# Prompt attention of a hybrid decoder step: a looped pass per KV head becomes one unrolled run of sixteen query tiles, and the softmax factors move from the transposes to the closed sums

## The reference, cut to what matters

```python
o_c, p_grp = compressed_attention(q, kc, vc, pos)     # 63 summary blocks, those that end before the token
o_s = selected_prompt(q, kv_s, idx, pos)              # 16 selected blocks of 64: with 1024 tokens, all of them
o_w = window_prompt(q, kv_w)                          # the last 512 tokens, a band
o = gates[..., 0:1] * o_c + gates[..., 1:2] * o_s + gates[..., 2:3] * o_w
```

## Time and profile before

| what | value |
|---|---|
| median of 3 runs | 3282.19 us (3277.84 to 3283.11) |
| the profiled execution, its own time | 3281.28 us |
| its span in the profile | 3279.6 us |
| TensorE busy in the span | 2924.5 us, 89% |
| VectorE, ScalarE, GpSimd busy | 44%, 28%, 9% |
| the stage that changes, first turn to last addition | 474.8 us, from 1623.5 to 2098.3 |
| its granted TensorE clock, mean | 0.86 |

### The profile page before, as it was taken

The page is one execution under the profiler, slowest core; times in us unless marked ns, Lnnn a source line. Parts: engine busy times, 40 slices in busy tenths (PEclk is TensorE's granted clock), DMA queues, the critical chain, the costliest instruction groups (busy, mean ns, idle before and its releaser), DMA issues. The chain is left out here.

```text
span 3279.6 us, 48743 instructions
## 1 busy us (share of the span) xinstructions
PE 2924.5 (89%) x18374; PEld 2688.3 (82%) x18374; DVE 1448.3 (44%) x2808; ACT 905.5 (28%) x1537; POOL 311.1 (9%) x294
## 2 busy tenths in 40 slices
PE   4999989999999997885789789687799999999997
PEld 4889879999999996884667667433589999999996
DVE  4444455544444445013255456312326454444445
ACT  4665651111111102111245345233222111111112
POOL 3444410000000001000011011211000000000000
PEclk9999999999999998997579879888899999999999
DMA  4212133211111102102100000365322111111101
GB/s 158 110 56 110 62 105 105 64 38 38 40 50 42 47 0 87 33 26 77 35 1 1 2 1 1 125 183 158 112 58 62 42 53 49 38 38 51 38 13 53
DMA packets 168574, 193.84 MB, mean 59 GB/s; under 512 B 11431, under 2 KB 154536, under 8 KB 165679
## 3 DMA queue, kind: packets, MB, share of 16 engines
q1 hardware_dynamic: 161623, 141.58, 14.2%
q0 software_dynamic: 6816, 50.49, 4.2%
HBM read 178.30 MB, written 17.91 MB: 60 GB/s over the span
## 5 line engine op out<-in xcount | busy, mean ns | idle before, releaser
L407 ACT ACTIVATE f_act_gate<-f_act_gate 128x352 f32<-128x352 f32 x132 | 65.8, 498 | 1186.2 <-DVE f_act_gate L464 1186.1
L501 DVE SCALAR_TENSOR_TENSOR trunk<-f_down,trunk 128x352 f32<-128x352 f32 x528 | 275.8, 524 | 207.8 <-PE f_down L104 207.8
L102 PE MATMUL f_up<-f_h_hi,f_gu_hi 128*128 128x352 f32 x1056 | 344.6, 326 | 0.0
L102 PE MATMUL f_gate<-f_h_hi,f_gu_hi 128*128 128x352 f32 x1056 | 344.3, 326 | 0.0
L104 PE MATMUL f_up<-f_h_hi,f_gu_lo 128*128 128x352 f32 x1056 | 342.8, 325 | 0.0
L104 PE MATMUL f_gate<-f_h_hi,f_gu_lo 128*128 128x352 f32 x1056 | 342.5, 324 | 0.0
L102 PE MATMUL f_down<-f_a_hi,f_wd_hi 128*128 128x352 f32 x1056 | 340.6, 323 | 0.0
L103 PE MATMUL f_gate<-f_h_lo,f_gu_hi 128*128 128x352 f32 x1056 | 340.5, 322 | 0.0
L103 PE MATMUL f_up<-f_h_lo,f_gu_hi 128*128 128x352 f32 x1056 | 340.1, 322 | 0.0
L103 PE MATMUL f_down<-f_a_lo,f_wd_hi 128*128 128x352 f32 x1056 | 338.5, 321 | 0.0
L104 PE MATMUL f_down<-f_a_hi,f_wd_lo 128*128 128x352 f32 x1056 | 338.1, 320 | 0.0
(11 more groups left out here) (333 smaller groups left out, 5812.3 us busy)
## 6 DMA issues: line engine op xcount, KB each, us to landing
as_pages<-in_cache_kv_slc_dram SPq DMA_DIRECT2D x192, 128.0 KB, 2.3
f_gu_raw<-in_w_ffn_gate_dram SPq DMA_DIRECT2D x44, 512.0 KB, 4.5
f_gu_raw<-in_w_ffn_up_dram SPq DMA_DIRECT2D x44, 512.0 KB, 5.7
f_wd_raw<-in_w_ffn_down_dram SPq DMA_DIRECT2D x22, 1024.0 KB, 5.0
as_pages<-in_cache_kv_slc_dram POOLq DMA_DIRECT2D x64, 128.0 KB, 3.2
in_w_raw<-in_w_in_dram SPq DMA_DIRECT2D x4, 1304.0 KB, 5.9
x_saved<-trunk SPq DMA_DIRECT2D x1, 4224.0 KB, 16.2
trunk<-x_saved SPq DMA_DIRECT2D x1, 4224.0 KB
```

What stands on the lines that cost most here:

```text
L102: pe.matmul(out, w_hi, x_hi, start=first, stop=False)
L407: act.activation(act_gate[:, b, :], act_gate[:, b, :], ACT.Silu).then_inc(silu_done, 1)
L501: dve.scalar_tensor_tensor(xT[:, m, chunk(c)], down_bank[n % 4][:, 0:CH], 0.5, xT[:, m, chunk(c)], ALU.mult, ALU.add).then_inc(down_free, 1)
```

## The change

The stage is written out for all sixteen tiles `n = 8 g + qt` (`TILES`) without a loop; waits have constant values and the `nop`s are gone. Beyond that:

- **Turns without factors.** A value turn is a transpose of `probs` with the identity. `diag` and GpSimd's `diagonals` are gone, and so is the wait for them.
- **Branches summed apart.** The products of the selected, window and compressed units of a tile go to `out_bank[(3 n + b) % 2]`, each closed on its own. Each closed sum is multiplied by its factors with VectorE (`scale`, one 128x512 product for each branch) into `scaled`, and GpSimd adds the three and the two halves into `mixT` (`gather`). `take_upper` and `take` are gone.
- **Factor rows.** The factors are per query, but in the closed sums queries lie along the free axis. `factors` is done once for a tile in the first head step of the next one; the 12 factors are split high and low (`factor_split`), transposed to 24 rows (turn `("f", n, None)`), and for each branch `b` four matmuls with `pick` (built once by GpSimd) spread the right rows over all partitions (turn `("f", n, b)`), which ScalarE copies to `spread`. These four turns a tile go through the same two turn banks. They stand in the first head step of the next tile (at its end) and at the head of its steps 1, 2 and 3.
- **Order.** A head's selected scores are issued at the end of the head step before, then comes the first turn of the step with the product still pending, then the window scores, then the other turns. ScalarE does the window exponentials after all the turns of the step. VectorE does the first `low` between the two maxima.
- **The seam.** The key and query turns of the second KV head alternate with the first units of tile 7 (`lead`), and the rest of tile 7's units lie in the head steps of tile 8.

```diff
-                with pe.Fori(0, N_KV) as g:
+    def lead(n):
+        own = [("k", n, b, half) for b in range(2) for half in range(2)] + [("q", n)]
+        values = quarter(n - 1, 0) if n else []
+        mixed = [x for pair in zip(own, values) for x in pair]
+        return mixed + own[len(values):]
+
+    def turns(n, r):
+        own = [("q", n + 1)] if r == 2 and n + 1 < TILES and not leads(n + 1) else []
+        if n == 0:
+            return own
+        values = [] if r == 0 and leads(n) else quarter(n - 1, r)
+        if r == 0:
+            return values + [("f", n - 1, None)]
+        return [("f", n - 1, r - 1)] + own + values
+
+    def head(xs):
+        return xs[:1] if xs and xs[0][-1] is not None else []
...
+                def gather(n):
+                    g, qt = divmod(n, QT)
+                    pool.wait_ge(scaled_done, 3 * n + 2)
+                    pool.tensor_tensor(scaled[:, 0], scaled[:, 0], scaled[:, 1], ALU.add).then_inc(added, 1)
+                    pool.wait_ge(scaled_done, 3 * n + 3)
+                    pool.wait_ge(added, 4 * n + 1)
+                    pool.tensor_tensor(scaled[:, 0], scaled[:, 0], scaled[:, 2], ALU.add).then_inc(added, 1)
+                    pool.wait_ge(added, 4 * n + 2)
+                    pool.tensor_copy(upper[:], scaled[HD:2 * HD, 0]).then_inc(added, 1)
+                    pool.wait_ge(added, 4 * n + 3)
+                    for half, sem in enumerate((added, out_taken)):
+                        pool.tensor_tensor(mixT[half * HD:(half + 1) * HD, 2 * g:2 * g + 2, qt * P:(qt + 1) * P],
+                                           scaled[0:HD, 0, half::2, :], upper[:, half::2, :], ALU.add).then_inc(sem, 1)
...
+                        for x in first:
+                            high(x)
+                        if n < TILES:
+                            exp_selected(n, r)
+                        for x in rest:
+                            high(x)
+                        if n < TILES:
+                            exp_window(n, r)
...
+                def scale(n, b):
+                    dve.wait_ge(pv_done, products[("v", n, ends[n][b])] + 1)
+                    dve.wait_ge(hi_done, at[("f", n, b)] + 1)
+                    if n:
+                        dve.wait_ge(out_taken, n)
+                    dve.tensor_tensor(scaled[:, b], out_bank[(3 * n + b) % 2][:].rearrange("p (r n) -> p r n", r=GROUP),
+                                      spread[:, b], ALU.mult).then_inc(scaled_done, 1)
...
                         for h in range(GROUP):
-                            tr = pe.matmul(bank[0:rows, h * P:(h + 1) * P], probs[qt % 2][:, h, lo:lo + rows],
-                                           diag[:, qt % 2, h, branch, :], start=True, stop=True)
+                            tr = pe.transpose(bank[0:rows, h * P:(h + 1) * P], probs[n % 2][:, h, lo:lo + rows],
+                                              K["ident"][:])
...
+                        _, n, b = x
+                        pe.wait_ge(hi_done, at[("f", n, None)] + 1)
+                        if n == 0 and b == 0:
+                            pe.wait_ge(pick_ready, 1)
+                        for h in range(GROUP):
+                            tr = pe.matmul(bank[:, h * P:(h + 1) * P], pick[:, 3 * h + BRANCHES[b], :], factor_rows[:],
+                                           start=True, stop=True)
...
+                def through(x):
+                    turn(x)
+                    value_product()
+                    if x[0] == "v":
+                        pending.append(x)
+
+                for n in range(TILES + 1):
+                    for r in range(GROUP):
+                        xs = turns(n, r)
+                        first = lead(n) if r == 0 and leads(n) else head(xs)
+                        rest = xs if r == 0 and leads(n) else xs[len(first):]
+                        for x in first:
+                            through(x)
+                        if r == 0 and leads(n):
+                            selected_scores(n, r)
+                        if n < TILES:
+                            window_scores(n, r)
+                        for x in rest:
+                            through(x)
+                        following = (n, r + 1) if r + 1 < GROUP else (n + 1, 0)
+                        if following[0] < TILES and not (following[1] == 0 and leads(following[0])):
+                            selected_scores(*following)
+                value_product()
```

More of the change, by code:

```diff
@@ L1608, in value_units @@
                 + [(CMP, CMP0, NB, None)])
[L1610 to L1637, removed]
+    def quarter(n, r):
+        count = len(value_units(n))
+        return [("v", n, u) for u in range(count * r // GROUP, count * (r + 1) // GROUP)]
@@ new lines, in head @@
+    def head(xs):
+        return xs[:1] if xs and xs[0][-1] is not None else []
+    order = [x for n in range(TILES + 1) for r in range(GROUP)
+             for x in (lead(n) if r == 0 and leads(n) else []) + turns(n, r)]
+    at = {x: i for i, x in enumerate(order)}
+    dups = {x: i for i, x in enumerate([x for x in order if x[0] in "kq"])}
+    dup_order = list(dups)
+    values_order = [x for x in order if x[0] == "v"]
+    products = {x: i for i, x in enumerate(values_order)}
+    ends = [[max(u for u, unit in enumerate(value_units(n)) if unit[0] == branch) for branch in BRANCHES]
+            for n in range(TILES)]
@@ L1639, in stage_attend_prompt @@
+    behind = {}
+    for x, follower in zip(values_order, values_order[1:]):
+        if x[2] in ends[x[1]]:
+            behind[follower] = (x[1], ends[x[1]].index(x[2]))
     with ExitStack() as scope:
@@ new lines, in _ @@
+                for x in dup_order[:5]:
+                    duplicate(x)
+                pool.tensor_tensor(pick[:], K["ident"][0:2 * ROWS, 0:ROWS].unsqueeze(2).to_broadcast([2 * ROWS, ROWS, P]),
+                                   K["ident"][0:2 * ROWS, ROWS:2 * ROWS].unsqueeze(2).to_broadcast([2 * ROWS, ROWS, P]),
+                                   ALU.add).then_inc(pick_ready, 1)
+                for n in range(TILES):
+                    if leads(n + 1):
+                        gather(n - 2)
+                    for x in dup_order:
+                        if x[1] == n + 1:
+                            duplicate(x)
+                    if n >= 2 and not leads(n + 1):
+                        gather(n - 2)
@@ L1714, in _, with high @@
+                for n in range(TILES - 2, TILES):
+                    gather(n)
             @block.scalar
             def _(act):
[L1716 to L1722 removed]
+                def high(x):
+                    i = at[x]
+                    bank = turn_bank[i % 2]
+                    act.wait_ge(turned, i + 1)
@@ L1950, in value_product @@
+                    pe.matmul(bank[:], values, turned_lo[v % RING][0:rows, :], start=False,
                               stop=last).then_inc(pv_done, 1)
[L1951 to L1973 removed]
```

456 lines of the change are left out of this document (227 added, 229 removed).

## The result

The kernel after takes 3297.53 us (median; 3295.34 to 3300.45), the kernel before in the same job 3282.44 (3277.84 to 3285.51). The ratio is 1.0046, 95% interval 1.0032 to 1.0059: slower by 0.46%, where the forecast was 0.6% faster (3261 for 3281.3). The profiled execution took 3296.15 with a span of 3294.0.

A forecast was written before the change was run, and what follows sets the result against it. The prediction took the stage to be bound by the round trip through three engines, or TensorE's queue behind scores. Full tiles -12, small tiles 0, seam -17, tail -3, clock +12 gave -20 from 3281.3: 3261 us, range 3240 to 3300.

The forecast's parts named there:

- The clock: Whole stage: more falls to 1.2 GHz, 36 us in all at 0.33 each, +12 us (bounds 0 and +50).
- the full tiles: Tiles 4 to 7, both passes: shorter round trips and turns, no `diag` wait, -12 us (bounds -16 and +4).
- rival 1: Stage: the clock takes the gain back once 97 us more run at 1.2 GHz; +24, 3305 us; chance 0.18.
- three signs that were named for an error upward: Stage: mean clock under 0.76, factor turns near 0.9 us, or a window score waiting for the window exponentials.
- Small tiles: Tiles 1 to 3, both passes: order's cost paid back by shorter turns and no `diag` wait, 0 (bounds -6 and +6).
- Factor turns: TensorE, sixteen tiles: three groups of four narrow matmuls at 0.47 us each and single transposes at about 0.15, 25 us.
- The seam: Last head step of the first pass to the second pass's tile 1: 49 us, -17 (bounds -24 and -9).
- The tail: Stage's end: 14 units, five factor turns, last scale and `gather` in 30.3 us, -3 (bounds -6 and +2).

The follow-up runs named there:

- u1_loop_only: The kernel before with only its loop over the two heads written out; 3261.00 us, ratio 0.9942.
- s1_seam_only: u1_loop_only plus the overlapped seam, five `nop`s gone, with the old diagonal matrices and step order kept; 3240.11 us, ratio 0.9877.
- h1_filled: The kernel after with extra products of keys with keys where TensorE waits, six or ten a step, changing the output; 3272.59 us, ratio 0.9975.
- g2_late_filled: g1_factors_late plus products of a zero matrix with the keys where TensorE waits; 3247.14 us, ratio 0.9908.
- d1_double_turns: The kernel after with every value transpose issued twice into the same place; 3291.34 us, ratio 1.0040.
- g1_factors_late: The kernel after with factor instructions behind the first step's lows and their turns at the second step's head and end; 3269.88 us, ratio 0.9973.
- s2_seam_filled: s1_seam_only plus five zero-matrix products in each tile's first step and every step of tiles 1 to 3 and 8 to 11; 3234.34 us, ratio 0.9861.

## Why the prediction was wrong

It forecast -20 and the profiles show +14.4, 34.4 us apart. The clock is 21.5 of them and the full tiles are 8.7. The wide range, 3240 to 3300, does hold 3297.5, but what happened there is rival 1, a loss, which had a chance of 0.18. By its own steps:

- *The clock* is the step that failed, by its size. I took 36 us more at 1.2 GHz at 0.33 each, +12. Outside the seam it is 90.5 us more (38.9, 44.3 and 7.3 in the ledger), and at 0.37, which two pairs of tiles with the same instructions give, that is +33, still inside the bounds of 0 and +50 that the term had. Rival 1 had the mechanism. It needed 97 us more; 57 were enough, since the other terms came to -21 (below), not -32. I had seen the wait of 2.5 us in the first step and set it down as a reason, but gave it "about half of the eight full tiles for some 7 us" and "a few more in the small ones". Six of the eight fell, and not for 7 us but for 17.1 (tile 4), 10.2 (tile 5) and 3.4 (tile 7), which is 44.3 more than before, and the small tiles have 38.9 more. I had looked at tile 7's first step; the long falls came in the tiles 3, 4 and 5, where scores are shorter and the units a larger share of the work (that this is the reason no run shows). None of the three signs that were named for an error upward showed: the stage's mean clock is 0.79 and not under 0.76, factor turns cost 0.58 and not 0.9, and window scores wait 2.1 us in all for exponentials.
- *Full tiles*, -12: +13.1, of which 44.3 x 0.37 = 16.4 are the clock, so -3.3. Tile 6, at 1.00 in both, says the same: -0.6, not -1.6. Its steps were forecast at 7.9, 6.1, 7.7 and 6.7 and are 8.51, 6.27, 7.93 and 6.72. Three of four hold within 0.25; the first misses by 0.6, mainly because the factor instructions take 1.99 us on VectorE, not the 1.1 scaled from a group of three. The first of them alone has 0.58, where 0.16 was the row. This is the second step that failed.
- *Small tiles*, 0: +17.8, of which 38.9 x 0.37 = 14.4 are the clock, so +3.4, inside its bounds.
- *Factor turns*: the four narrow matmuls cost TensorE about 0.58 at full clock, start to start, for 0.47 taken. A small part. Nor did `pick` matter: it has 1536 elements a partition and took 2.74 us once, where I had reckoned with 3072 and 5.9.
- *The seam*, -17: right, -20.2, and by its parts: the last head step and the eight alternating turns are 19.6 us for 20 (1833.47 to 1853.02), tile 8 is 26.9 for 25 and a share of the 4 for the clock. Half of it comes from the unrolled loop (57.0 for 66.6 in u1_loop_only), half from the mixed order, with the `nop`s gone (46.9 in s1_seam_only).
- *The tail*, -3: +1.7, of which 2.7 are the clock, so -1.0. The units ran at the forecast pace. The end did not: behind the last product stand a scale and GpSimd's five instructions, 2104.62 to 2109.55, 4.9 us where the sum had 3.5, and the next stage's first loads wait for them. One of these then took 1.69 us to issue for 0.43 in the kernel before; one execution does not tell whether that belongs to the change. The first TensorE instruction comes 13.95 us after the last product, where it was 9.6.

GpSimd and its five instructions at the end of the stage and the slow load of the next one, kernel after:

```profile
2104.62 1.26 POOL L1706 TENSOR_TENSOR at_scaled<-at_scaled 128x512 f32<-128x512 f32 x1 [20.84 <-DVE at_scaled L1840]
2104.70 0.69 DVE L1840 TENSOR_TENSOR at_scaled<-at_out_bank,at_spread 128x512 f32<-128x512 f32 x1 [0.22 <-PE at_out_bank L2023]
2106.03 1.26 POOL L1709 TENSOR_TENSOR at_scaled<-at_scaled 128x512 f32<-128x512 f32 x1
2107.35 0.61 POOL L1711 COPY at_upper<-at_scaled 64x512 f32<-64x512 f32 x1
2108.04 1.51 POOL L1714 TENSOR_TENSOR trunk<-at_scaled,at_upper 64x256 f32<-64x256 f32 x2
...
2111.02 1.69 SPq L2641 DMA_DIRECT2D new_mask<-const_new_mask_dram  x1
```

So -3.3 + 3.4 - 20.2 - 1.0 = -21.1 apart from the clock outside the seam, +33.5 for that clock, and +2.0 in the rest of the span: +14.4. Shown by runs: that work in TensorE's waits gives the time back (h1_filled, g2_late_filled), that it need be neither useful work nor matmuls (d1_double_turns), and that the place of the factor group changes the clock of whole tiles, to 1.00 in the tiles 5 and 7 of both passes and in one tile 4, though not in the small ones (g1_factors_late). Only worked out, not shown: the split of each part into clock and the rest, which hangs on one price. Kernels whose instructions differ give 0.29 to 0.44 for the same price (0.15 in s2_seam_filled, where fills stand outside the waits), and at these ends the clock outside the seam would be +26 to +40. Left open is what the new units lose in the small tiles even with late factors and fills (143.8 us for 133.2, with 19 us more low); no run takes the longer trip of the factor turns apart from the order of the step there. Open too is how the 57 us between s1_seam_only and the kernel after divide between the new units and the new order inside a step.

## What to carry to other kernels

Where TensorE's granted clock is not 1.00 throughout, a transformation that takes work from TensorE without shortening the waits between may not be a gain in full, and here was a loss. Price the clock for every tile and not from one: here 68 of the 90.5 us more at 1.2 GHz came in the tiles 3 to 5, and none in tile 7's first step, from which the price was taken. Tiny dependent instructions on VectorE (here five in 1.99 us) belong behind whatever the busiest engine waits for; here that gave back 27.7 us. And a change of several parts should be run in its parts: here the unrolled loop and the overlapped seam were worth -42 us, and the rest +57.

## What the runs showed of the hardware

- Issuing each of 592 value transposes a second time cost 2.3 us in tile 6 at full clock and nothing in the end (3291.3 for 3297.5 us), as the low time fell from 210.5 to 109.2 us.
- Products with a zero matrix hold the clock as well: 184.1 us of low time with none, 106.6 with them.
- One and the same tile of one execution took 32.18 and 25.06 us, with the same instructions, at a granted clock of 0.70 and 1.00.
